# Layer 1's attention: the next tile's query halves turned one at a time, each in front of a unit's scores

## What is computed

```python
q, k, v = jnp.split(h @ p['w_in'], 3, axis=-1)
q = rms_norm(q.reshape(B, L, 2, C_HEADS, HEAD_DIM), p['q_gain'])
k = rms_norm(k.reshape(B, L, 2, C_HEADS, HEAD_DIM), p['k_gain'])
...
s = jnp.einsum('bqphd,bsphd->bphqs', qblk, k, preferred_element_type=jnp.float32) * scale
pr = jax.nn.softmax(s, axis=-1)
w = (pr[:, 0] - lam * pr[:, 1]).astype(v.dtype)
return jnp.einsum('bhqs,bshe->bqhe', w, v)
```

## Time and profile before

| | us |
|---|---|
| median of 3 runs | 3421.89 |
| lowest, highest | 3421.48, 3423.62 |
| the profiled execution, first to last instruction | 3419.5 |
| TensorE busy in it | 3177.1 |
| VectorE busy | 2256.5 |
| ScalarE busy | 1874.9 |
| GpSimd busy | 626.3 |

### The profile page before, as it was taken

How to read it: one execution, slowest core, us unless ns; L and a number is a source line. 1 busy time by engine, 2 the same in 40 slices (tenths; PEclk the granted TensorE clock), 3 DMA queues, 4 the chain that set the end, 5 groups by cost and what they waited for, 6 DMA issues and landing times. The chain is left out here.

```text
span 3419.5 us, 55558 instructions
## 1 busy us (share of the span) xinstructions
PE 3177.1 (93%) x20138; PEld 2458.6 (72%) x20138; DVE 2256.5 (66%) x2851; ACT 1874.9 (55%) x2659; POOL 626.3 (18%) x482
## 2 busy tenths in 40 slices
PE   6988989998999999998899999999897999999999
PEld 4767777784667676765788888888885676776766
DVE  4667676546666666665677676867746666666666
ACT  3545746523565666664466483755723556665654
POOL 1211010000222332221201111011100123322231
PEclk9989999997999999999999999999997999999999
DMA  6230000238888888886010100100145688888885
GB/s 224 86 127 20 1 22 1 85 132 333 305 298 289 301 286 292 287 300 196 24 41 8 41 1 8 41 7 22 41 145 203 241 289 300 285 295 283 304 287 160
DMA packets 214171, 565.37 MB, mean 165 GB/s; under 512 B 33699, under 2 KB 71272, under 8 KB 213736
## 3 DMA queue, kind: packets, MB, share of 16 engines
q1 hardware_dynamic: 203614, 529.21, 43.2%
q0 software_dynamic: 9472, 33.57, 4.3%
q10 hardware_dynamic: 906, 0.23, 0.0%
HBM read 524.00 MB, written 38.94 MB: 165 GB/s over the span
## 5 line engine op out<-in xcount | busy, mean ns | idle before, releaser
L1976 DVE TENSOR_TENSOR moe_lo<-moe_raw,moeg_hi 128x2048 fp32r<-128x2048 f32 x384 | 880.4, 2327 | 322.9 <-PE psum L2344 154.9
L1973 ACT CAST moeg_hi<-moe_raw 128x2048 fp32r<-128x2048 f32 x384 | 728.9, 1910 | 413.3 <-PE psum L2362 291.6
L1042 PE MATMUL psum<-attn_w_hi,attn_hs 128*128 128x256 f32 (+2 forms) x1440 | 376.5, 346 | 27.0 <-PEq L2640 12.4
L1519 DVE TENSOR_REDUCE attn_neg_max<-psum 128x1 f32<-128x1280 f32 (+1 forms) x216 | 292.3, 1355 | 86.7 <-PE psum L1147 86.4
L1307 ACT ACTIVATE attn_e<-psum,attn_neg_max 128x1280 f32<-128x1280 f32 (+1 forms) x216 | 265.4, 1229 | 77.6 <-DVE attn_neg_max L1519 59.3
L1147 PE MATMUL psum<-attn_ks,attn_qst 128*128 128x512 f32 (+2 forms) x1200 | 284.2, 370 | 17.2 <-ACT attn_qst L1244 6.5
L1042 PEld LDWEIGHTS psum<-attn_w_hi,attn_hs 128*128 128x128 f32 x1440 | 256.7, 192 | 58.5 <-issue 19.6
L2362 PE MATMUL psum<-moeg_hi,moeh_x_hi 128*128 128x512 f32 x960 | 265.2, 398 | 4.8 <-issue 4.8
L2362 PE MATMUL psum<-moe_lo,moeh_x_hi 128*128 128x512 f32 x960 | 262.6, 395 | 0.0
L2362 PE MATMUL psum<-moeg_hi,moeh_x_lo 128*128 128x512 f32 x960 | 261.1, 393 | 0.0
L1147 PEld LDWEIGHTS psum<-attn_ks,attn_qst 128*128 128x128 f32 x1200 | 211.4, 191 | 63.7 <-issue 12.3
(11 more groups left out here) (345 smaller groups left out, 5433.4 us busy)
## 6 DMA issues: line engine op xcount, KB each, us to landing
moe_raw<-in_l_w_gate SPq DMA_DIRECT2D x256, 512.0 KB, 4.0
moe_raw<-in_l_w_up SPq DMA_DIRECT2D x256, 512.0 KB, 5.2
moe_raw<-in_l_w_down SPq DMA_DIRECT2D x128, 1024.0 KB, 6.2
ada_w<-in_l_ada_w SPq DMA_DIRECT2D x23, 1024.0 KB, 13.7
ada1h_w<-in_l_ada_w SPq DMA_DIRECT2D x9, 1024.0 KB, 10.8
lru_ada<-in_l_ada_w SPq DMA_DIRECT2D x8, 1024.0 KB, 6.5
lru_late<-in_l_ada_w SPq DMA_DIRECT2D x8, 1024.0 KB, 11.5
out_w<-in_l_w_out SPq DMA_DIRECT2D x16, 512.0 KB, 5.3
```

Source lines behind the costliest of these rows:

```text
L1042: last = pe.matmul(out, hs[t % 2][:, part, k, :], right, start=(i == 0 and n == 0), stop=(i == KB - 1 and n == 2))
L1519: dve.tensor_reduce(neg_max[:, n:n + 1], m.psum[:, score_at(n):score_at(n) + hi - lo], AX.X, ALU.max, negate=True).then_inc(s["maxed"], 1)
L1973: act.copy(mm.hi[slot % 4][:, :, :], mm.raw[slot][:, :, :]).then_inc(mm.s["hi_ready"], 1)
L1976: dve.tensor_tensor(mm.lo[slot][:, :, :], mm.raw[slot][:, :, :], mm.hi[slot % 4][:, :, :].bitcast(F32), ALU.subtract).then_inc(mm.s["lo_re ...
```

## The change

In layer 1 the staging of tile 1 stays where it was, in pass 0. From pass 2 on a staging is no longer one step of eight turns behind the scores of map 0 in each even pass. It is two steps of four turns, half `u % 2` of tile `u // 2 + 1` as the first thing in pass u, in even and odd passes alike, up to pass 15. ScalarE's two reads stand in the same places of its queue. `scores` of a tile's first unit waits in layer 1 for the half of its own map, in layer 0 for both as before. `q_split` is now waited for before each half. VectorE does `split_queries(u // 2 + 2)` at the end of odd passes instead of even ones, since `qq` is free only when half 1 has been turned. The count of instructions that compute is the same.

```diff
@@ program
+            if l == 1 and u >= 2 and u // per_tile + 1 < NT:
+                make["stage_half"](u // per_tile + 1, u % per_tile)
             if l == 1 and u + 1 < units:
                 make["scores"](u + 1, 0)
-            if l == 1 and u % per_tile == 0 and u // per_tile + 1 < NT:
-                make["stage"](u // per_tile + 1)
+            if l == 1 and u == 0:
+                make["stage"](1)
@@ tensor
+                staged = {}
+
+                def stage_half(qt, half):
+                    pe.wait_ge(s["q_split"], j * NT + (qt + 1))
+                    at = next_turn()
+                    for i in range(2):
+                        flat = qq[:, 2 * half + i, :, :].rearrange("p v d -> p (v d)")
+                        for v in range(2):
+                            last = pe.transpose(m.psum[:, at + (2 * i + v) * P:at + (2 * i + v + 1) * P],
+                                                flat[:, v * HD:v * HD + P], m.ident[:, :])
+                    last.then_inc(s["turned"], 1)
+                    staged[qt, half] = turn[0]
+
                 def stage(qt):
-                    pe.wait_ge(s["q_split"], j * NT + (qt + 1))
                     for half in range(2):
...
+                        stage_half(qt, half)
@@ tensor, scores
-                        if u % per_tile == 0 and i == 0:
-                            pe.wait_ge(s["turn_read"], j * TURNS + staged[u // per_tile])
+                        if u % per_tile == 0 and l == 1:
+                            pe.wait_ge(s["turn_read"], j * TURNS + staged[u // per_tile, which])
+                        if u % per_tile == 0 and l == 0:
+                            pe.wait_ge(s["turn_read"], j * TURNS + staged[u // per_tile, 1])
@@ scalar
+                def stage_half(qt, half):
+                    read_turn(qst[qt % 2][:, 2 * half:2 * half + 2, :, :].rearrange("p n v t -> p (n v) t"), 4 * P,
+                              groups_of=("p (n t) -> p n t", dict(t=P)))
@@ vector
-                    if l == 1 and u % 2 == 0 and u // 2 + 2 < NT:
+                    if l == 1 and u % 2 == 1 and u // 2 + 2 < NT:
                         split_queries(u // 2 + 2)
```

## The result

| | before | changed | ratio, 95% interval |
|---|---|---|---|
| first comparison, median us | 3421.68 | 3454.41 (3445.11 to 3454.54, 4 runs) | 1.0097 [1.0084, 1.0111] |
| second, beside other kernels | 3417.55 | 3446.55 (3444.74 to 3451.96, 4 runs) | 1.0090 [1.0073, 1.0107] |
| span of the profiled execution, first | 3419.5 | 3452.7 | |

What follows compares the result with a forecast made beforehand. It took TensorE, busy for 93% of the span, to bound the kernel, idling mainly on a chain over three engines. Three groups at +7.0 us and one at +6.2 gave +27 us: 3449 us, range 3438 to 3460.

Steps and rivals of the forecast that it cites:

- The chain behind S0 and the split: In odd passes query turns wait for VectorE's late split: odd 7.84 us, even 6.20, pair 14.04 against 13.28, +0.76.
- The signs: In layer 1's attention: 28 split waits of 0.8 to 1.6 us, 14.0 us between first halves, granted clock 1.00.
- No gain even with the queries ready: In steady pairs, even without the split wait, a chain over three engines would hold the pair at 13.2 us.
- the chain over ScalarE that I named: Scores, maxima, exponential, query-half read, turns: lets the next pass go past its first half 8.65 us behind first scores.
- Waits per map: In pass 1, first scores wait only for half 0's read and may start one ScalarE read earlier (0.53 us).
- Layer 0 and the repeated waits: Repeated split waits cost nothing for half 1 and in layer 0; at 0.05 us in some 50 places, 2 us.
- The start of a group: Up to pass 3's first scores: first split wait ends at 1744.7, those scores come 0.29 us later than before.
- the low clock as a rival for all 28 stalls: Rival: TensorE's clock falls too, at stalls in 28 pairs, at most 42 us more, 3491 us; chance 0.04.
- The end of a group: Through the last passes: +6.2 us in the last group, +7.0 in the three that also convert the next group's tokens.
- I carry the lag through: After pass 15's value products the work is unchanged, so the delay of 7.0 or 6.2 us lasts.
- the token term: In pass 12 of three groups, token conversion delays the next maximum 2.22 us, into the split wait: +1.6 us.
- Sum: Whole kernel: 3 x 7.0 + 6.2 = 27 us; 3419.5 + 27 + 2.4 = 3449 us, +0.8%; chance 0.81.

Runs made afterwards that it cites:

- e1: Changed kernel with VectorE's split of the next tile's queries in front of the odd pass's first maximum instead of behind its second: 3422.09 us, ratio 1.0003.
- e5: e1 with ScalarE's map 1 exponential and normalisation put behind the read of the next pass's query half: 3408.67 us, ratio 0.9975.
- e3: Kernel before with only the change's per-map waits (map 0 scores wait for half 0, map 1 for half 1): ratio 1.0007.
- e8: Changed kernel with only each group's first moved split (tile 2's) back at the end of pass 0: 3442.95 us, ratio 1.0061.
- e9: Changed kernel with tile 2's split back in pass 0 and the next tokens' cast and subtraction in pass 13 instead of 12: 3438.83 us, ratio 1.0049.

## Why the prediction was right, point by point

Forecast 3449 us (+27 us, 3438 to 3460); measured 3454.4, and 3446.6 in a second comparison.

**The chain behind S0 and the split.** Right, part by part: second maximum 4.90 behind S0 as in the sum, split 1.40 after it, turns 1.11 after that instead of 1.03; half and S0 behind the wait 0.41 (1790.97 - 1790.56) instead of 0.50. These two misses cancel, which is luck. Odd slot 7.82 against 7.84, even slot 6.21 against 6.20, pair 14.03 against 14.04. In the last group the turns come 1.04 behind the split's start and the pair is 13.96 (2432.04 - 2418.08) where it was 13.29, +0.67: that, over five pairs, is the 0.4 us by which this group stays under its 6.2.

**The signs.** The wait for the split came 28 times, and P0's wait for a query read in odd slots alone, as written. But its length was to be 0.8 to 1.6 us each, and 17 of the 28 are of 0.5 to 0.6, the others 0.8 to 1.3 at slot 4 and 2.2 to 2.5 at slot 2 and slot 14. The short ones are a matter of counting: from start to start the steady stall is (1790.56 - 1787.59) - (1782.79 - 1780.56) = 0.74 us, V to half with and without the wait, and the profile counts only from the modelled end of the products. The long ones follow from the prediction's own sum: it had the first split wait end at 1744.7, and 1747.00 - 2.21, the later start of the group, is 1744.8. That TensorE would by then have stood idle for 2.5 us it did not write down, and the clock depended on it.

**No gain even with the queries ready.** Shown by e1: 13.24, where I had worked out 13.2. e5 shows that it is the chain over ScalarE that I named: with one link of it moved, the pair is 12.86.

**Waits per map.** Shown to be nothing by e3. **Layer 0 and the repeated waits:** nothing is seen of them behind the scatter ahead of the stretch.

**The start of a group.** +0.29 us at S0 of slot 3 in the forecast. In the fourth group it is (2396.78 - 2379.51) - (2369.18 - 2352.12) = +0.2: right. In the first group it is (1755.09 - 1736.14) - (1750.98 - 1733.93) = +1.9. The difference is TensorE's clock. First group, behind the wait of 2.5 us at the head of slot 2 (start, length, row):

```profile
1747.00 0.98 PE L1123 MATMUL psum<-ident,attn_qq 128*128 128x128 f32 x4 [2.48 <-DVE attn_qq L1485]
1747.64 2.48 PE L1154 MATMUL psum<-attn_ks,attn_qst 128*128 128x512 f32 x6
1749.91 1.37 PE L1167 MATMUL psum<-ident,attn_e 128*128 128x128 f32 x8
1751.04 1.41 PE L1154 MATMUL psum<-attn_ks,attn_qst 128*128 128x512 f32 x6
```

and the fourth group, the same products behind a wait of 2.3 us:

```profile
2390.29 0.66 PE L1123 MATMUL psum<-ident,attn_qq 128*128 128x128 f32 x4 [2.32 <-DVE attn_qq L1485]
2390.70 1.40 PE L1154 MATMUL psum<-attn_ks,attn_qst 128*128 128x512 f32 x6
2391.94 1.04 PE L1167 MATMUL psum<-ident,attn_e 128*128 128x128 f32 x8
2392.74 1.40 PE L1154 MATMUL psum<-attn_ks,attn_qst 128*128 128x512 f32 x6
```

From the half to the second scores it is 4.04 us there and 2.45 here. The windows of these places, of slot 14 in the first group and of the steady part (length, busy us and count of PE, PEld, DVE, ACT, POOL, granted clock, DMA):

```profile
1746.90:1751.04 4.14, 4.04 (x19) 3.66 (x19) 0.89 (x1) 1.27 (x4) 0.00 (x0) 0.59 0.00 0
2390.30:2393.90 3.60, 3.60 (x24) 3.26 (x25) 1.68 (x3) 2.38 (x6) 0.00 (x0) 1.00 0.00 0
1835.20:1839.20 4.00, 3.98 (x18) 3.66 (x19) 1.45 (x2) 1.74 (x5) 0.00 (x0) 0.59 0.00 0
1755.00:1824.00 69.00, 62.93 (x462) 57.28 (x460) 53.27 (x76) 54.85 (x117) 6.79 (x19) 1.00 0.00 1
```

0.59 is part of the window at 1.2 GHz and part at 2.4, 1.00 is 2.4 throughout. This is the term that was mis-sized: I had the low clock as a rival for all 28 stalls (+42 us) and as one more fall a group in the upper bound. It came only behind the two long waits of a group, those of slot 2 and slot 14, twice in each of three groups. The stalls of the steady pairs, two of 0.6 us in each as the profile counts them, left it at 1.00 over 69 us. The Trainium skill, TensorE: Matmul & The Clock Gate, section "HAM oscillation — how this bites in real kernels", says that waits between bursts of products can put the engine to its lower clock again and again. By these rows that happened here behind long waits, not behind each of them, and not behind the short ones. In the second profile of the changed kernel the clock fell again at slot 2 of the first group, and not behind the same 2.2 us wait at slot 14:

```profile
1740.00:1744.00 4.00, 3.85 (x19) 3.62 (x20) 1.60 (x4) 1.74 (x4) 0.00 (x0) 0.68 0.00 0
1828.30:1832.00 3.70, 3.60 (x24) 3.26 (x25) 1.89 (x4) 2.67 (x7) 0.00 (x0) 1.00 0.00 0
```

so a wait of this length may or may not cost it, from one execution to the next. Over the twelve profiles there are 25 waits of 2.2 to 2.5 us at slot 2 or 14, and behind 16 of them the clock fell; between slots 4 and 13 it fell in no group of any profile. That the long wait is the cause is read from this and from e8, where the wait at slot 2 is gone and no fall comes there; no run changes the clock by itself.

**The end of a group.** Lengths from first staging to first staging (the last to the output turns), changed against before: +8.4, +9.6, +7.3 us, and +5.8 for the last; forecast 7.0 three times and 6.2. The lag at V of slot 15, in the first group (1846.44 - 1736.14) - (1834.77 - 1733.93) = 9.5, and at the group's end:

| group | 1 | 2 | 3 | 4 |
|---|---|---|---|---|
| first profile, at V of slot 15 | 9.5 | 9.4 | 8.2 | 5.8 |
| first profile, at the end | 8.4 | 9.6 | 7.3 | 5.8 |
| second profile, at V of slot 15 | 8.7 | 8.0 | 6.5 | 5.8 |
| second profile, at the end | 8.0 | 9.1 | 5.5 | 5.8 |

"I carry the lag through" holds in the last group, to 0.1 us. What the first and third groups seem to give back belongs to the kernel before, whose own clock falls at the end of these two groups, in the first at 1848 us and in the third twice, at slot 14 and at the end (windows of the kernel before, columns as above):

```profile
2240.50:2243.50 3.00, 3.00 (x12) 2.62 (x11) 1.03 (x1) 2.14 (x4) 0.00 (x0) 0.50 0.00 0
2261.00:2264.00 3.00, 3.00 (x8) 2.35 (x8) 1.33 (x4) 2.14 (x4) 0.67 (x2) 0.50 0.39 117
```

The changed kernel's first profile has none there; its second has one, at the end of the second group, and there the lag grows from 8.0 to 9.1. The sum for a group with tokens can be read from the first group of the second profile, whose only fall is that at slot 2: 8.7 less 1.6 is 7.1, forecast 7.0. e9 against e8 does not measure the token term by itself: the 2.5 us between their stretches contain falls of the clock at different places. In the second group, where neither has one up to V of slot 15, the tokens' move is worth (2051.29 - 1943.74) - (2047.70 - 1941.74) = 1.6 us there.

**Sum.** The forecast's 27 us, 27.2 unrounded, are 31.0 and 28.5 in the two profiles. An estimate from the rows above closes both. A fall at slot 2 costs 1.6 us. One at slot 14 costs 0.8 (9.5 against 8.7 at V of slot 15 in the first group, both with the same lag at slot 13). The three falls of the kernel before are worth 1.1 and 0.9 at the two ends and 1.2 in the third group's slot 14 (9.4 against 8.2). First profile: 27.2 + 3 x 1.6 + 3 x 0.8 - 3.2 = 31.2. Second, with one fall at slot 2, two at slot 14 and one at an end: 27.2 + 1.6 + 1.6 + 1.1 - 3.2 = 28.3. So the waits were sized right, and the clock is what the number missed: the 27 counts neither the falls behind the changed kernel's long waits nor the three of the kernel before, which do not come back with the change, and the ones in part cancel the others. Of the 32.7 us between the medians 31.0 are in the stretch; the rest is within what the beginning of the stretch scatters.

## What to carry to other kernels

Before a step is put at the head of a slot of an in-order queue, work out when its input is ready in that slot, not only how long it takes: here 0.41 us of turns stood in front of everything, and their input was one of the last things that the other engine made in the slot before. A wait named in a profile can be the visible end of a chain that leads over three engines; another order of the same turns moves the place of the wait and not its length, and only cutting the chain (here: the exponential behind the read) made it shorter. When a loss is found, try the producer's other idle time before undoing the edit: the split fitted into 1 us of idle VectorE, and with the held exponential the kernel is 0.25% faster than before.

## What the runs showed that I had not expected

- TensorE's clock fell to its lower level behind single waits of 2.2 to 2.5 us in otherwise busy stretches, and with the same wait it sometimes did not; one fall at slot 2 cost 1.6 us (4.04 against 2.45 for the same products), one at slot 14 about 0.8 by V of slot 15. The kernel before has three such falls in the stretch too, so a comparison of two profiles has to count them on both sides.
- The time ahead of layer 1's attention differs by 9.8 us between executions of instructions that are the same but for repeated waits, more than any of the smaller effects here. The stretch of interest, read from the trace, sets that aside: the two profiled executions of the changed kernel are 9.8 us apart as a whole and 2.5 in the stretch.
- In e5 TensorE is busy without a gap from 1747.6 to 1811.8 us, ten slots on end, though each of its slots is 0.2 us longer than TensorE's work in it. The weight loads of the second scores wait 0.34 us there, and the modelled ends of the turns ahead of them cover the gap. So full busy time is not yet the shortest slot; the distance from start to start shows it. Its window (columns as above):

```profile
1747.60:1811.80 64.20, 64.20 (x472) 58.62 (x471) 54.84 (x75) 53.61 (x119) 7.39 (x20) 1.00 0.01 1
```
